# Index scores of a sparse-attention layer: three passes over padded keys become two stacked passes, woven with the strip products

## The chip, the cores and the metric

One core of a Trainium2 chip runs the whole kernel. The metric is the device time of one execution in microseconds (us), from the median of several runs. The tensor engine is TensorE (PE in the profile, its weight loads PEld), the vector engine VectorE (DVE), the scalar engine ScalarE (ACT), the general engine GpSimd (POOL), and SyncE (SP) only issues transfers. SBUF is the on-chip memory, PSUM the accumulators: 8 banks of 512 float32 columns by 128 partitions.

## The reference, cut to what matters

The kernel computes two layers of an encoder for 1024 tokens with a model width of 1024. Layer 1 has sparse attention. An indexer gives each query a score for each key, and the 256 best keys are attended. This document is about the indexer:

```python
q_idx = partial_rope(q_idx.reshape(b, s, IDX_HEADS, IDX_DIM), positions)   # 16 heads x 64
k_idx = partial_rope(k_idx, positions)                                     # one key of 64
idx_logits = relu(einsum('bqhd,bsd->bqhs', q_idx, k_idx))
score = einsum('bqh,bqhs->bqs', w_idx, idx_logits) * IDX_SCALE
score = where(visible, score, -inf)
top_val, top_idx = lax.top_k(score, topk)                                  # topk = 256
```

Each head's 1024 x 1024 logits pass a ReLU, are weighted by a number per query and head, and are summed over 16 heads. The projections ahead of it multiply x (1024 x 1024) with weight strips of 128 columns: 8 strips for `q_idx` (two heads each), one for the key, two for the latent key and value, a narrow one for the weights. After top-k come 32 strips of the attention's own queries ("q strips"), a value projection, and the attention.

## The kernel before, in words

All products are bf16 with float32 accumulation. For accuracy each float32 operand is split into a high bf16 part and a low bf16 rest, and a product is made of three passes: high x high, low x high, high x low. A strip product (`products`, L302) is 8 contraction tiles x 3 passes x 2 halves of 512 columns = 48 matmuls and fills two PSUM banks. Weights come in pieces of 512 KB through four slots: SyncE loads `w_stage`, GpSimd splits it into `w_hi` and `w_lo` (L272, L275), TensorE uses it. The order on each engine is written out by hand, one program per engine and phase, tied by counting semaphores.

Layer 0 is one block of phases. Its last phase ("dn0", down projection and second norm) also computes the small strips of layer 1 (key, two latent strips, weights) while it waits for the norm. Then the semaphores are cleared behind a barrier of all engines (`clear_sems`, L176), and layer 1 is a second block: index, top-k, attention, output projection and norm, feed-forward. In the index phase:

- SyncE loads the rotary tables (L1467) and then the weight pieces of the eight index strips and of the first four q strips.
- ScalarE takes each strip out of PSUM: four copies of 32 rows, exchanged in pairs, into `strip_w` (L1456) and one of 128 rows into `strip_f` (L1457). VectorE multiplies both by the tables and adds them (L1561, L1562, L1565). ScalarE writes the high part (L1533), VectorE the low part (L1584). There is one `strip_f` and one `strip_w`, so the copy of a strip waits for the low part of the strip before.
- The key's high and low parts are held twice, once per head of a strip, each with zeros in the 64 rows of the other head.
- Only when all strips are rotated does TensorE begin the scores. There are 96 steps: 8 strips x 2 heads x 6 query blocks of 128 (blocks 2 to 7; the first two see no more than 256 keys). Block i has (i + 1) x 128 key columns, so 384 to 1024. A step has three passes (L1501) into one of four pairs of banks, a ReLU on ScalarE (L1541) from PSUM into `strip_f` or `strip_w`, and on VectorE one instruction that multiplies by the weight and adds into `score` (L1595). TensorE waits for the ReLU of four steps before, ScalarE for the add of two steps before.
- Strips 1 to 7 of the score steps run in a hardware loop.

In the top-k phase VectorE finds 8 maxima per row and step and replaces them, 32 times (L1786, L1790), and writes the masks `hide`. Beside it TensorE computes the 32 q strips and then 16 value chunks of 6 matmuls (L1688), whose high parts ScalarE and whose low parts VectorE takes out of PSUM (L1739, L1807). A value chunk from the ninth on waits for a low part of an earlier chunk. The first latent scores of the attention (L1872) follow.

## Time and profile before

| | us |
|---|---|
| median of 3 timed runs | 3090.5 |
| lowest and highest | 3088.91 and 3095.48 |
| profiled execution, its time | 3094.27 |
| profiled execution, its span | 3092.5 |
| TensorE busy in the span | 2916.7 (94%) |
| VectorE busy | 1828.5 (59%) |
| ScalarE busy | 1030.8 (33%) |
| GpSimd busy | 1452.6 (47%) |
| mean granted TensorE clock | 0.984 |

The span runs from the first to the last instruction; the execution's time is a little longer. "Busy" is the time with at least one instruction in work. Matmuls are pipelined, so a matmul is shown longer than the distance to the next. The granted clock is a share of full speed: 1.0 is 2.4 GHz and 0.5 is 1.2 GHz, and a mean between them is a mixture. The index phase lies at about 1381 to 1622 us of the span.

### The profile page before, as it was taken

The page shows a single profiled execution, that of the slowest core. Times are in us where ns is not written, and L with a number is a line of the kernel's source. Part 1 is how long each engine was busy: PE and PEld are TensorE (multiplying, and loading weights), DVE is VectorE, ACT ScalarE, POOL GpSimd, SP SyncE. Part 2 cuts the span into 40 slices and gives each one's busy share as a digit, 9 for nine tenths or more (in the row PEclk, how much of TensorE's full clock was granted, in tenths as well). Part 3 has the DMA queues.
Part 4 walks back from the last instruction along what each step waited for, and adds up shares of the span by engine and source line. Part 5 has one row for each costly group of instructions (what it writes and reads, how often), then busy time and mean ns, then how long its engine had stood idle before and what let it go on. Part 6 is the DMA issues. An engine that isn't in the chain of part 4 may idle for free.

```text
span 3092.5 us, 45889 instructions
## 1 busy us (share of the span) xinstructions
PE 2916.7 (94%) x17190; PEld 1514.4 (49%) x17472; DVE 1828.5 (59%) x2540; ACT 1030.8 (33%) x1671; POOL 1452.6 (47%) x721
## 2 busy tenths in 40 slices
PE   7999997999999999977789999999999999999998
PEld 4566655444444444443344444577764444444443
DVE  5877556574444473155589999777757644444042
ACT  3655667022222210014563343566640222221000
POOL 4677211654343378825106777500017534343885
PEclk9999999999999999998899999999999999999999
DMA  4222221411111133311002222111112111111322
GB/s 137 56 65 67 58 59 28 178 55 48 54 47 54 48 109 123 102 36 68 27 0 96 109 102 88 69 55 54 54 68 77 60 54 47 54 47 61 110 96 101
DMA packets 96516, 218.24 MB, mean 71 GB/s; under 512 B 41328, under 2 KB 41456, under 8 KB 96416
## 3 DMA queue, kind: packets, MB, share of 16 engines
q1 hardware_dynamic: 54048, 195.74, 17.9%
q10 hardware_dynamic: 42368, 21.11, 2.9%
q8 instruction: 70, 1.15, 0.1%
q14 instruction: 30, 0.25, 0.0%
HBM read 176.92 MB, written 23.12 MB: 65 GB/s over the span
## 4 chain that ended last, share of the span: by engine, by line
PE 44%; DVE 5%; ACT 4%; issue 1%; POOL 1%; DMA 0%; DVEq 0%; POOLq 0%; ACTq 0%; SPq 0%
PE ps L302 24%; PE ps L313 8%; PE ps L1872 5%; PE ps L1908 2%; DVE score L1595 1%; PE ps L1887 1%; ACT strip_w L1541 1%; PE ps L337 1%; ACT strip_w L1456 1%; PE ps L1688 1%; POOL w_hi L272 0%; DVE strip_f L1565 0%; DVE strip_w L1562 0%; DVE x_res L1224 0%; POOL w_lo L275 0%
## 5 line engine op out<-in xcount | busy, mean ns | idle before, releaser
L272 POOL TENSOR_TENSOR w_hi<-w_stage,ones 128x1024 bf16<-128x1024 f32 x227 | 460.6, 2029 | 908.7 <-PE ps L302 539.9
L302 PE MATMUL ps<-xt_hi,w_hi 128*128 128x512 bf16 x1888 | 566.0, 380 | 33.8 <-ACT strip_f L1457 29.6
L302 PE MATMUL ps<-xt_lo,w_hi 128*128 128x512 bf16 x1889 | 565.7, 380 | 1.6
L302 PE MATMUL ps<-xt_hi,w_lo 128*128 128x512 bf16 x1880 | 563.8, 380 | 2.1
L275 POOL TENSOR_TENSOR w_lo<-w_stage,w_hi 128x1024 bf16<-128x1024 f32 x227 | 525.3, 2314 | 17.8
L302 PEld LDWEIGHTS ps<-xt_hi,w_hi 128*128 128x128 bf16 x1920 | 187.6, 98 | 259.5 <-issue 29.3
L302 PEld LDWEIGHTS ps<-xt_lo,w_hi 128*128 128x128 bf16 x1920 | 187.9, 98 | 227.8 <-issue 1.9
L302 PEld LDWEIGHTS ps<-xt_hi,w_lo 128*128 128x128 bf16 x1920 | 187.8, 98 | 227.4 <-issue 1.1
L1224 DVE SCALAR_TENSOR_TENSOR x_res<-x_res,ps 128x1024 f32<-128x1024 f32 x32 | 38.9, 1216 | 359.5 <-PE ps L313 359.5
L1354 DVE TENSOR_SCALAR conv_up<-gate_up,conv_w_up 128x1024 f32<-128x1024 f32 x44 | 78.4, 1782 | 280.0 <-ACT gate_up L1335 279.4
L313 PE MATMUL ps<-w_hi,hid_hi 128*128 128x512 bf16 x689 | 206.4, 379 | 5.6 <-DVE x_res L1224 4.0
L313 PE MATMUL ps<-w_lo,hid_hi 128*128 128x512 bf16 x690 | 206.6, 379 | 0.7
L313 PE MATMUL ps<-w_hi,hid_lo 128*128 128x512 bf16 x690 | 206.4, 379 | 0.7
L1872 PE MATMUL ps<-lat_hi,q_now 128*128 128x512 bf16 (+3 forms) x729 | 185.6, 323 | 1.2
L1192 ACT ACTIVATE ln_rstd<-ln_rstd 128x1 f32<-128x1 f32 x32 | 6.5, 203 | 524.0 <-DVE ln_rstd L1233 524.0
L1790 DVE MATCH_REPLACE8 score<-best,score 128x384 f32<-128x384 f32 (+2 forms) x192 | 165.7, 876 | 0.0
L1786 DVE MAX8 best<-score 128x8 f32<-128x384 f32 (+2 forms) x192 | 155.5, 879 | 3.3
L1366 DVE TENSOR_TENSOR hid_lo<-conv_up,hid_hi 128x1024 f32 x44 | 115.8, 2633 | 59.5 <-ACT hid_hi L1339 59.5
L898 POOL TENSOR_TENSOR prob<-take,prob 128x1024 f32<-128x1024 f32 (+3 forms) x64 | 107.0, 1677 | 87.5 <-DVE prob L877 71.1
L1996 POOL COPY v_now_hi<-val_hi 128x512 bf16 (+1 forms) x16 | 9.8, 613 | 270.6 <-PE ps L1887 253.3
L694 DVE TENSOR_TENSOR pt_lo<-ps,pt_hi 128x512 bf16<-128x512 f32 x192 | 100.1, 548 | 55.9 <-ACT pt_hi L688 55.7
L673 PE MATMUL ps<-ident,prob 128*128 128x128 f32 x576 | 89.8, 281 | 43.8 <-DVE pt_lo L694 40.5
(230 smaller groups left out, 5757.4 us busy)
## 6 DMA issues: line engine op xcount, KB each, us to landing
w_stage<-in_l_up SPq DMA_DIRECT2D x88, 512.0 KB, 3.2
w_stage<-in_l_down SPq DMA_DIRECT2D x88, 512.0 KB, 3.2
w_stage<-in_l_o SPq DMA_DIRECT2D x32, 512.0 KB, 3.9
w_stage<-in_l_q SPq DMA_DIRECT2D x32, 512.0 KB, 4.6
q_split<-q_out SPq DMA_DIRECT2D x32, 512.0 KB, 2.6
q_now<-q_split SPq DMA_DIRECT2D x16, 1024.0 KB, 4.8
w_stage<-in_l_qkv SPq DMA_DIRECT2D x24, 512.0 KB, 3.3
k_twice<-nk_hi ACTq DMA_DIRECT2D x32, 128.0 KB, 2.9
```

What stands on the lines that cost most here:

```text
L272: pool.tensor_tensor(w_hi[slot][:, 0:cols], w_stage[slot][:, 0:cols], ones[:, 0:1].to_broadcast([P, cols]), ALU.mult).then_inc(w_cast[slot ...
L275: pool.tensor_tensor(w_lo[slot][:, 0:cols], w_stage[slot][:, 0:cols], w_hi[slot][:, 0:cols], ALU.subtract).then_inc(w_split[slot], 1)
L302: mm = pe.matmul(ps[:, bank + h, :], w, a[:, k, h * HALF:(h + 1) * HALF], start=(first and k == k0 and m == 0), stop=(last and k == k1 - 1 ...
L313: mm = pe.matmul(ps[:, bank + h, :], a[:, k, rows], w[slot][:, h * HALF:(h + 1) * HALF], start=(k == 0 and m == 0), stop=(k == tiles - 1 a ...
L673: mm = pe.transpose(dst, self.prob[t % 4][:, cols], ident[:, :])
L694: dve.tensor_tensor(lo, src, hi, ALU.subtract).then_inc(self.lo, 1)
L898: pool.tensor_tensor(prob[t % 4][:, 0:n], take[t % 4][:, 0:n], prob[t % 4][:, 0:n], ALU.mult).then_inc(s_wsb, 1)
L1354: dve.tensor_scalar(conv[a][:, :], gate[a][:, 0:SEQ], tap(0), tap(3), ALU.mult, ALU.add).then_inc(s_cv, 1)
L1366: dve.tensor_tensor(hid_lo[:, m, :], conv[a][:, :], hid_hi[:, m, :], ALU.subtract).then_inc(s_hl, 1)
L1786: dve.max(best[:, c, :], score[:, sc_at[i]:sc_at[i] + span[i]]).then_inc(s_top, 1)
L1790: dve.match_replace(cell, best[:, c, :], cell, TAKEN_SCORE).then_inc(s_rep, 1)
L1872: mm = pe.matmul(ps[:, 2 * (t % 2) + c // 512, 0:w], a, b, start=(kt == 0 and m == 0), stop=(kt == 1 and m == 2))
```

## The change

- The barrier and the clearing of semaphores between the layers go, and both layers are one block. The norms' semaphores are made once and shared, and each norm phase waits for values with its own offset (`at`, `phases_done`). SyncE waits for the sixteenth residual add (`s_acc`) before it loads the tables.
- The exchange of 32-row parts is no longer done by four copies out of PSUM. ScalarE copies the strip once into one of two `strip_f` and then issues four SBUF-to-SBUF transfers from its own queue into one of two `strip_w` (two for the latent strip). The product with the sine table moves to GpSimd. The cosine product and the sum are done by VectorE in the PSUM banks of the strip.
- The key is held once, high and low, with its 64 rows in both halves of the partitions. A query strip is held per head as one tile of 128 rows: the head's 64 high rows in their place and its 64 low rows in the other half. One pass with the key's high part gives high x high + low x high, and a second with the key's low part the rest. Two buffers of query strips stay instead of eight.
- Strips and scores are woven: product s, then the twelve steps of strip s - 2, and so on. The last two groups have q strip 0 between them and q strip 1 behind them. Copy, rotate, highs and lows of a strip stand at set places among the ReLUs and adds of the strip before.
- The strips use banks 4 to 7, the steps banks 0 to 3 in two pairs. ReLU is done in PSUM, the add reads PSUM, and a step's matmuls wait for the add of two steps before. The first six adds write `score` instead of adding to it. Loops are unrolled. `strip_unit` is one of the eight contraction tiles of a strip product, six matmuls as in `products`; `strip_bank(s)` is 4 or 6, and `strip_lows` counts two low parts per strip.
- In the top-k phase the q strips use the banks in the order 4, 6, 0, 2, only strips 2 and 3 are left of the first four, the value chunks' banks are shifted by four for the first eight, and chunk 8 waits for five low parts, chunk 9 for six, and so on.

```diff
+        s_gb, s_blk, s_acc = sem("gb_loaded"), sem("block_done"), sem("accumulated")
-                    pe.wait_ge(s_b, i + 1)
+                    pe.wait_ge(s_b, TB * at + i + 1)
...
-        clear_sems()
...
+        qi = [[room(f"qi{b}{hh}", [P, SEQ], BF16) for hh in range(2)] for b in range(2)]
+        ki_hi, ki_lo = [room(n, [P, SEQ], BF16) for n in ("ki_hi", "ki_lo")]
+        strip_f = [room(f"strip_f{b}", [P, SEQ], F32) for b in range(2)]
+        strip_w = [room(f"strip_w{b}", [P, SEQ], F32) for b in range(2)]
+        IDX_STEPS = 2 * len(picky)
+        Q_BANK = (4, 6, 0, 2)
+        SMALL_LOWS = 3
+        def idx_step(g):
+            s, t = g // IDX_STEPS, g % IDX_STEPS
+            return s, t // len(picky), picky[t % len(picky)], 2 * (g % 2)
...
         def index_sync(sp):
+            sp.wait_ge(s_acc, TB * 2)
         def index_gpsimd(pool):
+            def sine(w, tab, b, swapped):
+                pool.wait_ge(s_sw5[b], swapped)
+                pool.tensor_tensor(w, w, tab, ALU.mult).then_inc(s_s5, 1)
+            split_piece(pool, feed_qidx, 0, 0)
+            pool.wait_ge(s_tl5, 64)
+            sine(strip_w[0][:, :], rope_i[1][:, :], 0, 64)
+            split_piece(pool, feed_qidx, 1, 0)
...
+            for s in range(KT):
+                sine(strip_w[s % 2][:, :], rope_i[1][:, :], s % 2, swaps_through(s))
+                if s < 4:
+                    split_piece(pool, feed_qidx, s, 1)
+                else:
+                    split_piece(pool, feed_q, s - 4, 0)
         def index_tensor(pe):
-                    products(pe, feed_qidx, r, i, 2 * ((r + 1) % 4), xt_hi, xt_lo, 0, KT, True, True)
-                        pe.wait_ge(s_ir, idx_steps * p + t - 3)
-                        for m, (a, b) in enumerate(((qi_hi, ki_hi), (qi_lo, ki_hi), (qi_hi, ki_lo))):
-                                           b[hh][:, c:c + w], start=(m == 0), stop=(m == 2))
+            def scores(g):
+                s, hh, i, bank = idx_step(g)
+                if g % IDX_STEPS == 0:
+                    pe.wait_ge(s_l5, strip_lows(s))
+                if g >= 2:
+                    pe.wait_ge(s_ia, g - 1)
+                for c in range(0, span[i], 512):
+                    w = min(512, span[i] - c)
+                    for m, keys in enumerate((ki_hi, ki_lo)):
+                        mm = pe.matmul(ps[:, bank + c // 512, 0:w], qi[s % 2][hh][:, i * P:(i + 1) * P],
+                                       keys[:, c:c + w], start=(m == 0), stop=(m == 1))
+                mm.then_inc(s_iq, 1)
+            for s in range(KT):
+                if s == 0:
+                    pe.wait_ge(s_l5, 1)
+                elif s == 1:
+                    pe.wait_ge(s_w5, 2)
+                else:
+                    pe.wait_ge(s_l5, strip_lows(s - 2))
+                for k in range(KT):
+                    strip_unit(pe, feed_qidx, s % 4, s // 4, strip_bank(s), k)
+                if s >= 2:
+                    for t in range(IDX_STEPS):
+                        scores(IDX_STEPS * (s - 2) + t)
+            for r in range(2):
+                pe.wait_ge(s_l5, strip_lows(KT - 2 + r))
+                for t in range(IDX_STEPS):
+                    scores(IDX_STEPS * (KT - 2 + r) + t)
+                for k in range(KT):
+                    strip_unit(pe, feed_q, r, 0, Q_BANK[r], k)
         def index_scalar(act):
+            def copy_strip(m, bank, b, heads, used, swapped, rotated):
+                act.wait_ge(*used)
+                wait_if(act, s_sw5[b], swapped)
+                act.activation(strip_f[b][:, :], banks(bank), ACT.Copy).then_inc(s_f5, 1)
+                act.wait_ge(s_f5, m + 1)
+                wait_if(act, s_a5, rotated)
+                for a in range(0, 64 * heads, 32):
+                    to = a + 32 if a % 64 == 0 else a - 32
+                    act.dma_start(strip_w[b][to:to + 32, :], strip_f[b][a:a + 32, :]).then_inc(s_sw5[b], 16)
...
+            def relu(g):
+                s, hh, i, bank = idx_step(g)
+                act.wait_ge(s_iq, g + 1)
+                act.activation(banks(bank)[:, 0:span[i]], banks(bank)[:, 0:span[i]], ACT.Relu).then_inc(s_ir, 1)
+            def highs(s):
+                act.wait_ge(s_a5, 2 + s + 1)
+                if s >= 2:
+                    act.wait_ge(s_iq, IDX_STEPS * (s - 1))
+                for hh in range(2):
+                    rows = slice(hh * IDX_DIM, (hh + 1) * IDX_DIM)
+                    act.activation(qi[s % 2][hh][rows, :], banks(strip_bank(s))[rows, :], ACT.Copy).then_inc(s_h5, 1)
+            for s in range(KT):
+                copy_strip(2 + s, strip_bank(s), s % 2, 2,
+                           (w_used[feed_qidx.slot(s % 4)], feed_qidx.used(s % 4, s // 4) + 1),
+                           swaps_through(s) - 64, s + 1)
+                for t in range(IDX_STEPS):
+                    if s >= 1 and t < 5:
+                        relu(IDX_STEPS * (s - 1) + t)
+                    if t == 4:
+                        highs(s)
+                    if s >= 1 and t >= 5:
+                        relu(IDX_STEPS * (s - 1) + t)
+            for t in range(IDX_STEPS):
+                relu(IDX_STEPS * (KT - 1) + t)
         def index_vector(dve):
+            def cosine(m, bank, rows, tab):
+                src = banks(bank)[0:rows, :]
+                dve.wait_ge(s_f5, m + 1)
+                dve.tensor_tensor(src, src, tab[0:rows, :], ALU.mult).then_inc(s_c5, 1)
+            def rotate(m, bank, rows, b):
+                src = banks(bank)[0:rows, :]
+                dve.wait_ge(s_c5, m + 1)
+                dve.wait_ge(s_s5, m + 1)
+                dve.tensor_tensor(src, src, strip_w[b][0:rows, :], ALU.add).then_inc(s_a5, 1)
...
+            def add(g):
+                s, hh, i, bank = idx_step(g)
+                cell, src = score[:, sc_at[i]:sc_at[i] + span[i]], banks(bank)[:, 0:span[i]]
+                w = w_idx[:, i, 2 * s + hh:2 * s + hh + 1]
+                dve.wait_ge(s_ir, g + 1)
+                if g < len(picky):
+                    dve.tensor_scalar(cell, src, w, None, ALU.mult).then_inc(s_ia, 1)
+                else:
+                    dve.wait_ge(s_ia, g - len(picky) + 1)
+                    dve.scalar_tensor_tensor(cell, src, w, cell, ALU.mult, ALU.add).then_inc(s_ia, 1)
+            def lows(s):
+                for hh in range(2):
+                    rows = slice(hh * IDX_DIM, (hh + 1) * IDX_DIM)
+                    other = slice((1 - hh) * IDX_DIM, (2 - hh) * IDX_DIM)
+                    dve.wait_ge(s_h5, SMALL_LOWS + 2 * s + hh + 1)
+                    dve.tensor_tensor(qi[s % 2][hh][other, :], banks(strip_bank(s))[rows, :],
+                                      qi[s % 2][hh][rows, :], ALU.subtract).then_inc(s_l5, 1)
+            for s in range(KT):
+                cosine(2 + s, strip_bank(s), P, rope_i[0])
+                for t in range(IDX_STEPS):
+                    if t == 3:
+                        rotate(2 + s, strip_bank(s), P, s % 2)
+                    if t == 7:
+                        lows(s)
+                    if s >= 1:
+                        add(IDX_STEPS * (s - 1) + t)
+            for t in range(IDX_STEPS):
+                add(IDX_STEPS * (KT - 1) + t)
...
+        def chunk_bank(c):
+            return (c + Q_BANK[0]) % 8 if c < 8 else c % 8
...
-            pe.wait_ge(s_ir, idx_steps * KT)
-                products(pe, feed_q, r, 0, 2 * r, xt_hi, xt_lo, 0, KT, True, True)
+            pe.wait_ge(s_ia, IDX_STEPS * KT)
+            for r in range(2, 4):
+                products(pe, feed_q, r, 0, Q_BANK[r], xt_hi, xt_lo, 0, KT, True, True)
+                    products(pe, feed_q, r, i, Q_BANK[r], xt_hi, xt_lo, 0, KT, True, True)
-                    pe.wait_ge(s_vl, c - 7)
+                    pe.wait_ge(s_vl, (c + Q_BANK[0]) % 8 + 1)
...
```

## Rows read from the trace of the kernel before

**Rows 1.** Busy time of each engine, granted clock and transfers in five stretches.

```profile
core 0: us, PE busy (x) PEld busy (x) DVE busy (x) ACT busy (x) POOL busy (x), PEclk, DMA share, GB/s
1381.20:1409.60 28.40, 0.00 (x1) 0.14 (x3) 18.82 (x11) 10.24 (x10) 17.49 (x7) 0.50 0.52 176
1409.60:1496.60 87.00, 85.05 (x382) 38.17 (x388) 42.74 (x30) 40.68 (x42) 36.13 (x16) 0.99 0.15 52
1496.60:1519.60 23.00, 3.70 (x12) 1.47 (x14) 9.62 (x8) 12.35 (x14) 3.33 (x2) 0.59 0.07 23
1519.60:1621.80 102.20, 91.60 (x458) 43.15 (x467) 87.15 (x96) 70.48 (x95) 0.00 (x0) 0.97 0.00 0
1621.80:1974.30 352.50, 351.08 (x1603) 159.35 (x1629) 340.66 (x607) 134.23 (x141) 243.21 (x110) 1.00 0.26 98
```

**Rows 2.** Chain of waits, 1370 to 1660 us: start, duration, work on it.

```profile
1383.77 6.92 DMA rope_q_sin<-rope_tables
...
1402.89 2.82 DVE ki_lo L1571
...
1409.60 11.61 PE ps L302 x47
...
1606.66 1.03 ACT strip_w L1541
1607.83 1.30 DVE score L1595
...
1619.33 1.03 ACT strip_w L1541
1620.41 10.04 PE ps L302 x38
```

**Rows 3.** Timeline of TensorE at the end of the value chunks: start, duration.

```profile
1974.11 0.38 PE L1688 MATMUL ps<-w_lo,lat_hi 128*128 128x512 bf16 x1
1974.33 0.38 PE L1872 MATMUL ps<-lat_hi,q_now 128*128 128x512 bf16 x1
```

**Rows 4.** ReLU (L1541), add (L1595) and residual add (L1224): durations in ns.

```profile
L1541 ACT ACTIVATE strip_f<-ps x48: 485/704/922, 1519.0 to 1618.1; 128x384 f32<-128x384 f32 x16, 128x640 f32<-128x640 f32 x16, 128x896 f32<-128x896 f32 x16
L1541 ACT ACTIVATE strip_w<-ps 128x1024 f32<-128x1024 f32 x16 | 16.4, 1024 | 8.4 <-DVE score L1595 6.8 <-PE ps L1501 1.6
L1595 DVE SCALAR_TENSOR_TENSOR score<-strip_w,w_idx,score x48: 744/1018/1287, 1520.2 to 1620.5; 128x512 f32<-128x512 f32 x16, 128x768 f32<-128x768 f32 x16, 128x1024 f32<-128x1024 f32 x16
L1224 DVE SCALAR_TENSOR_TENSOR x_res<-x_res,ps 128x1024 f32<-128x1024 f32 x32 | 38.9, 1216 | 359.5 <-PE ps L313 359.5
```

**Rows 5.** Transfers inside SBUF from ScalarE's queue: length of the issue, and landing.

```profile
L626 ACTq DMA_DIRECT2D k_twice<-nk_hi x32: 617/620/1867, 50.7 to 493.4; - x32
k_twice<-nk_hi ACTq DMA_DIRECT2D x32, 128.0 KB, 2.9
```

**Rows 6.** GpSimd by line and shape: count, busy us, mean ns.

```profile
L275 POOL TENSOR_TENSOR w_lo<-w_stage,w_hi 128x1024 bf16<-128x1024 f32 x226 | 524.9, 2323 | 17.8
L272 POOL TENSOR_TENSOR w_hi<-w_stage,ones 128x1024 bf16<-128x1024 f32 x226 | 459.2, 2032 | 908.7 <-PE ps L302 539.9 <-PE ps L313 227.7 <-PE ps L569 48.3
L1755 POOL TENSOR_TENSOR qs_w<-qs_w,rope_q_sin 64x1024 f32<-64x1024 f32 x16 | 37.6, 2352 | 193.9 <-ACT qs_w L1718 193.9
```

**Rows 7.** The stretches 502 to 538 us by engine, as rows 1.

```profile
502.00:510.00 8.00, 4.42 (x32) 3.19 (x34) 5.70 (x15) 7.55 (x18) 0.00 (x0) 1.00 0.00 1
510.00:514.00 4.00, 1.22 (x12) 0.84 (x9) 3.48 (x10) 3.75 (x10) 0.00 (x0) 1.00 0.41 66
514.00:518.00 4.00, 3.81 (x12) 1.81 (x14) 2.31 (x6) 1.95 (x5) 0.00 (x0) 0.57 0.00 0
524.00:538.00 14.00, 7.46 (x53) 5.23 (x55) 10.63 (x30) 13.42 (x32) 0.00 (x0) 1.00 0.00 1
```

**Rows 8.** Timeline of VectorE at the end of top-k.

```profile
1959.64 0.19 DVE L1803 MEMSET hide<- 64x64 bf16 x2
1959.75 4.44 DVE L1807 TENSOR_TENSOR val_lo<-ps,val_hi 128x512 bf16<-128x512 f32 x7
```

More of the change, by code:

```diff
@@ L1046, in back_and_norm @@
             b_rows = room(f"b_rows_{tag}", [P, D_MODEL], F32)
[L1047 to L1054 removed]
+            s_x = [sem(f"{tag}_x_loaded{g}") for g in range(2)] if load_x is not None else None
+            at = phases_done(tag)
+            s_out = sem(f"{tag}_stored") if final is not None else None
             tail = tiles - SLOTS
@@ L1449, in copy_strip @@
-        def copy_strip(act, bank, kind, wait_prev):
-            act.wait_ge(s_l5, wait_prev)
-            src = banks(bank)
-            swaps = {"idx": (0, 32, 64, 96), "lat": (0, 32), "plain": ()}[kind]
-            for a in swaps:
-                b = a + 32 if a % 64 == 0 else a - 32
-                act.activation(strip_w[b:b + 32, :], src[a:a + 32, :], ACT.Copy)
-            act.activation(strip_f[:, :], src, ACT.Copy).then_inc(s_f5, 1)
-        def strip_kind(m):
-            return "idx" if m == 0 or m >= 3 else ("lat" if m == 1 else "plain")
+        s_sw5 = [sem(f"strip_swapped{b}") for b in range(2)]
@@ new lines, in strip_unit @@
+        def strip_unit(pe, feed, n, i, bank, k):
+            slot = feed.slot(n)
+            if k == 0:
+                pe.wait_ge(w_split[slot], feed.use(n, i) + 1)
+            wh, wl = w_hi[slot][:, k * P:(k + 1) * P], w_lo[slot][:, k * P:(k + 1) * P]
+            for m, (w, a) in enumerate(((wh, xt_hi), (wh, xt_lo), (wl, xt_hi))):
+                for h in range(2):
+                    mm = pe.matmul(ps[:, bank + h, :], w, a[:, k, h * HALF:(h + 1) * HALF],
+                                   start=(k == 0 and m == 0), stop=(k == KT - 1 and m == 2))
+            if k == KT - 1:
+                mm.then_inc(w_used[slot], 1)
@@ new lines, in index_scalar, with low @@
+            for t in range(IDX_STEPS):
+                relu(IDX_STEPS * (KT - 1) + t)
+        def index_vector(dve):
+            def cosine(m, bank, rows, tab):
[7 more added lines that the diff above has]
+                dve.tensor_tensor(src, src, strip_w[b][0:rows, :], ALU.add).then_inc(s_a5, 1)
+            def low(dst, hi, bank, n):
+                dve.wait_ge(s_h5, n)
+                dve.tensor_tensor(dst, banks(bank), hi, ALU.subtract).then_inc(s_l5, 1)
+            dve.wait_ge(s_tl5, 64)
+            cosine(0, 0, P, rope_i[0])
+            cosine(1, 2, ROPE, rope_q[0])
+            low(lat_lo[:, 1, :], lat_hi[:, 1, :], 4, 1)
+            rotate(0, 0, P, 0)
+            rotate(1, 2, ROPE, 1)
+            low(ki_lo[:, :], ki_hi[:, :], 0, 2)
+            low(lat_lo[:, 0, :], lat_hi[:, 0, :], 2, 3)
+            dve.wait_ge(s_w5, 2)
+            def add(g):
[26 more added lines that the diff above has]
+                add(IDX_STEPS * (KT - 1) + t)
@@ L2022, in program @@
         run_phases(
+            *layer0,
             phase(index_sync, index_gpsimd, index_tensor, index_scalar, index_vector),
```

222 lines of the change are left out of this document (57 added, 165 removed).

## The prediction, made before the changed kernel had run

> **What bounds the kernel now.** I read the stage table of the index part first [rows 1]. TensorE has nothing to multiply from 1381.2 to 1409.6 us, works on the eight index products until 1496.6, stands for most of the next 23 us, and runs the 96 score steps until about 1619. Then come 352.5 us in which TensorE (the q strips) and VectorE (top-k) are both busy throughout. The chain of waits says why [rows 2]: the hole at 1381 is the table loads, issued only after the barrier, then the rotation of the key strip through one pair of SBUF buffers (the last low half is written at 1402.89 to 1405.7), and the first product only starts at 1409.60. The score steps are not limited by TensorE: ReLU and add follow each other, and twelve steps take 1619.33 - 1606.66 = 12.67 us.
>
> **Prices.** A 512-column matmul starts every 0.216 us and is shown 0.38 long [rows 3], so 0.165 is its tail. A product of 48 is 10.36 us. A ReLU is 0.485 us at 384 elements and 1.024 at 1024, linear between; the add is 1.285 at 1024 and 0.744 at 512 [rows 4]. Between engines 0.05 us passes where no register is stepped (1619.33 + 1.03 to 1620.41) and 0.11 to 0.14 where the loop does it [rows 2]. The new code has constants only, so I take 0.2 for the three hand-overs of a step (matmul to ReLU to add to matmul).
>
> **The change, part by part.**
>
> *The start.* No barrier, and the tables are loaded after the last residual add of the stage before, some 40 us earlier, so tables, weight pieces and the small strips' copies lie beside the small products. SyncE's queue holds only these loads and is moved past nothing else. On GpSimd the key strip's sine stands between the first two splits, which take 2.0 + 2.3 us each [rows 6]; with the first slot free from the small product at 1368 both are ready before products 0 and 1 need them at 1381 and 1392. Product 0 starts at 1381.2, where TensorE falls idle now. Gain: 28.4 us.
>
> *The first strip.* Product 2 waits for the low half of strip 0. From the end of product 0: copy 1.02, four DMA issues on ScalarE at 0.62 = 2.5, landing 2.9 [rows 5], sine on GpSimd 2.35 [rows 6], rotate 1.2, two highs 2.0, two lows 2.4, waits 0.4: 14 us. Product 1 covers 10.4 of them, so 3.6 are open. 1381.2 + 20.7 + 3.6 + 10.4 (product 2) = 1416.0, where the first group starts.
>
> *A group of twelve steps.* Passes go from three to two, and the stacked copies make the zero halves unnecessary. For TensorE a group is 2 x 8448 columns / 512 x 0.216 = 7.1 us, against 10.7 now. But banks fall from four to two: a step's matmuls wait for the add of two steps before, since ReLU and add now work in the bank itself. Behind that wait stand the rest of the group and the next product, and for these wait the copy of the next strip and everything after it. So one bank is a closed ring of matmul, ReLU and add. The odd bank has the larger sizes (512, 768, 1024, twice): matmuls 1.94 + 3 x 0.165 = 2.44, ReLUs 2.43, adds 3.05, waits 0.6, together 8.5, twice 17.0; the last ReLU and add (2.4) run beside the next product, which leaves 14.8. Inside the group lie a rotate on VectorE, two highs on ScalarE and two lows on VectorE of the following strip. Walked step by step, the rotate holds the add of step 3 back by 1.0 us, the highs hold the ReLU of step 5 by 0.6, the lows, which wait for the highs, the add of step 7 by 1.3. A group is 14.8 + 2.9 = 17.7 us, in which TensorE works 7.1. The four DMA issues, copy, cosine, sine and split fall into the product that follows and are hidden by its 10.4 us. GpSimd's splits don't slow the adds: the residual add, one input in PSUM, has 1216 ns on average over 32 with GpSimd busy beside many of them [rows 4].
>
> *The sum to the last add.* 1416.0; five times group and product, 5 x 28.05 = 140.3, 1556.3; group 5, 17.7; group 6 follows without a product, so the copy with its four DMA issues and the late sine of strip 7 are open: 17.7 + 5.1 = 22.8; q strip 0, 10.4; group 7 without insertions 14.8, 1622.0; last ReLU and add 2.4: 1624.4. Now it is 1620.5 + 1.29 = 1621.8 [rows 4]. So the hole at the start is given back inside the groups: a strip costs 28 us where product and steps cost 10.9 + 12.7 now.
>
> The norms' semaphores, now shared by both layers, change constants only and cost nothing.
>
> *Bounds of what rows 4 don't show.* An add that reads PSUM with a weight per partition: 1285 (SBUF, same form) or 1216 (PSUM, constant factor) at 1024. The lower one would give 4.4 us over all groups; I take the middle, 1622.2. A ReLU that writes PSUM is shown nowhere: the nearest is the same one into SBUF (1.024); lower bound is its column part alone, 0.86, upper bound the SBUF figure plus as much. I take 1.024.
>
> The Trainium skill, "VectorE: DVE Perf Modes", section on the TRN2 errata, gives VectorE a larger fixed cost for a PSUM source than for SBUF (120 against 58 cycles). That would be an estimated 65 ns per add and put the last add 2 us later. The trace does not bear it out: 1216 ns from PSUM against 1285 from SBUF.
>
> *The clock.* Over a whole group TensorE is shown busy 7.1 + 12 x 0.165 = 9.1 of 17.7 us. At such a share (7.46 of 14 us, 4.42 of 8) the granted clock stayed 1.00 [rows 7]. But around the lows (steps 6 to 8) it is 1.8 of 6 us, and after 1.22 of 4 us the clock was 0.57 [rows 7], so at 1.2 instead of 2.4 GHz for most of the stretch. I expect one fall per group. One fall costs what it costs at 1409.60: 11.61 us for a product of 10.36 [rows 2], 1.25 us. Eight are 10 us: last add at 1632.2.
>
> The Trainium skill, "TensorE: Matmul & The Clock Gate", section "HAM oscillation", says that dependence gaps in a loop return the clock to half each time round. That speaks against this change; the trace agrees with it in the fall after 1.22 of 4 us.
>
> *Top-k and values.* VectorE needs 1959.8 - 1621.8 = 338.0 us from the last add to the end of the hide masks [rows 8]. Before, TensorE ended last here (32 strips, 16 value chunks) and VectorE had some slack. Now two q strips are done early (one before and one behind the last group), so TensorE reaches value chunk 8 at 1629.7 + 31 x 10.36 + 8 x 1.295 = 1961. It waits there, as chunk 8 now takes the bank of chunk 4 and needs five lows of VectorE: 1632.2 + 338.0 + 5 x 0.634 [rows 8] = 1973.4. Eight chunks are 10.4, plus 1.5 for the clock after 12 us without work: the first latent score starts at 1985.3, where it is 1974.33 [rows 3]. Its order behind that point is the same. Difference: +11 us. The profiled execution has 3094.3 us (span 3092.5 and 1.8 around it), so 3105; it lay 3.8 above the median of the three timed runs, 3090.5. On their scale I forecast 3101.
>
> **The rivals.** 0.2% (6 us) is about what a measurement of this kernel can tell from no change.
> - *The clock holds* (chance 0.20): for it, 524 to 538 [rows 7]; against it, the 30% around the lows. Last add 1622.2, first latent score 1975.3, +1: 3091.5.
> - *Faster: the ring is shorter than SBUF rows say* (0.16). Place: ReLU and add of every step, both in PSUM. If the ReLU were at its lower bound and the add at 1216, and the clock held because the ring is shorter, the last add would be at 1613.7, first latent score at 1966.8, -7.5: 3083. It decides from a last add before about 1615. Against it: nothing in the rows is that short. The Trainium skill, "ScalarE: Activation LUTs", section "Step-by-step: what each stage is for", says that ScalarE writes PSUM faster than SBUF. It gives no figure, and no row here shows such a write; this rival is what it would bring at most.
> - *The clock stays at half through the groups* (0.12): all step matmuls at double length put the last add at 1648.7, and the sum at +28: 3118. Against it: busy shares of half held 1.00.
>
> **Numbers.** The forecast has 0.52 (own range 3096 to 3110). Slower by over 0.2%: forecast and third rival, less the lower edge, 0.60; within: 0.23; faster: 0.17. The range 3086 to 3114 leaves out part of the faster case and of the slowest.
>
> **What would show it.** Right: product 0 within 2 us of 1381; a repeat of about 28 to 29.5 us per strip; a score step's matmul released by VectorE's add; granted clock at half inside groups (mean under 0.9 over the stage); last add at 1628 to 1636; TensorE idle some 10 us in the value chunks. Wrong: a repeat under 27 us (ring too dear), clock at 1.00 throughout, a hole left at 1381, or a ReLU in PSUM well under 1.0 us.

## The result, and the profile after

The changed kernel takes 3107.61 us (median of 6 runs, 3103.43 to 3110.55) against 3094.88 us (6 runs, 3088.91 to 3095.85, the three of the table above among them) for the kernel before: a ratio of 1.0043, 95% interval 1.0030 to 1.0056. The ratio is an estimate over all runs; the two medians alone give 1.0041. The kernel is slower, by less than half a percent but clear of noise. The forecast was 3101.0, in a range of 3086 to 3114.

The profiled execution took 3108.03 us (span 3106.2, mean granted clock 0.977).

In what follows "product s" is the 48 matmuls of strip s, and a "group" is the twelve score steps of one strip; groups count from 0.

**One offset first.** The first normalization of layer 0, long before any changed work of the index stage, starts 3.3 us later in the profiled execution after than in that before. In the fourteen executions of this study (before, after, twelve experiments) this row starts between 577.2 and 586.0. With one profiled execution of the kernel before, nothing shows whether part of the 3.3 us belongs to the change. So I take 3.3 us off each time of the changed kernel ("aligned") and give the last add of each experiment as a distance from this row. Timeline of VectorE, first the kernel before, then the changed one; the row holds min, median and max in ns, then first and last start:

```profile
L1228 DVE BATCH_NORM_STATS2 ln_stats_o<-x_res x8: 676/685/695, 581.6 to 590.9; 128x6 f32<-128x512 f32 x8
```

```profile
L1222 DVE BATCH_NORM_STATS2 ln_stats_o<-x_res x8: 676/685/695, 584.9 to 594.2; 128x6 f32<-128x512 f32 x8
```

**By stretches** of the changed kernel, columns as in [rows 1]: small products' end; products 0 to 2; groups 0 to 4 with products 3 to 7; groups 5 to 7 with q strip 0; then q strips and top-k up to the first latent score.

```profile
1381.20:1384.70 3.50, 3.30 (x101) 2.87 (x100) 1.51 (x2) 1.19 (x3) 3.42 (x3) 1.00 0.00 0
1384.70:1419.67 34.97, 32.62 (x141) 14.32 (x143) 10.54 (x9) 6.30 (x8) 21.94 (x11) 0.95 0.30 91
1419.67:1566.17 146.50, 108.24 (x432) 43.41 (x440) 78.34 (x80) 58.63 (x75) 29.14 (x14) 0.83 0.13 36
1566.17:1637.40 71.23, 48.26 (x177) 17.58 (x180) 41.60 (x43) 32.51 (x43) 8.80 (x5) 0.76 0.08 22
1637.40:1987.05 349.65, 339.89 (x1542) 154.22 (x1572) 336.69 (x608) 133.13 (x140) 242.68 (x110) 0.99 0.26 99
```

The hole of [rows 1], 1381 to 1409, is gone: TensorE is busy 3.30 of the first 3.50 us and goes straight on. In its place the two stretches with the groups stand at a mean clock of 0.83 and 0.76, and a strip costs (1566.17 - 1419.67) / 5 = 29.3 us. A group, a product and a group in full, and the last group, which has nothing inserted:

```profile
1419.67:1439.26 19.59, 12.64 (x41) 4.42 (x41) 13.24 (x14) 9.69 (x13) 0.00 (x0) 0.66 0.08 27
1439.26:1449.64 10.38, 10.33 (x48) 4.59 (x47) 2.42 (x2) 2.03 (x2) 4.04 (x2) 0.99 0.22 51
1449.64:1468.26 18.62, 10.58 (x41) 3.88 (x41) 12.61 (x14) 9.70 (x13) 2.29 (x2) 0.82 0.08 28
1620.58:1635.04 14.46, 8.92 (x42) 3.19 (x41) 9.81 (x11) 7.85 (x11) 0.00 (x0) 1.00 0.00 1
```

Group 6, which follows group 5 with no product between them, ran at half clock for nearly its whole length:

```profile
1589.70:1610.20 20.50, 13.01 (x35) 4.36 (x37) 13.38 (x14) 9.64 (x13) 6.32 (x3) 0.50 0.15 43
```

What TensorE waited for between 1384.7 and 1640 (us in total, times, longest):

```profile
PE ps L1502 <- DVE score L1615: 55.6, 45, 3.0
PE ps L1502 <- DVE score L1612: 4.6, 4, 1.8
PE ps L1458 <- DVE qi L1622: 2.2, 1, 2.2
```

In a group, the score matmuls (L1502) are released by VectorE's add (L1615), not by the product or by ScalarE. The longest of these waits, 3.0 us, lies across the two lows (L1622, the subtractions that write the low parts of the next strip). There the clock falls. In TensorE's timeline of group 1 a 512-column matmul is 0.38 long before the wait (2.4 GHz) and 0.63 after it (1.2 GHz):

```profile
1456.48 0.38 PE L1502 MATMUL ps<-ki_lo,qi 128*128 128x512 bf16 x1
1457.06 0.33 PE L1502 MATMUL ps<-ki_lo,qi 128*128 128x384 bf16 x1
1460.41 0.63 PE L1502 MATMUL ps<-ki_lo,qi 128*128 128x512 bf16 x1 [3.02 <-DVE score L1615]
1460.83 0.63 PE L1502 MATMUL ps<-ki_hi,qi 128*128 128x512 bf16 x1
```

The durations that answer [rows 4] (ReLU now inside PSUM, add now from PSUM) and [rows 5] (the swap DMAs: issue, then landing):

```profile
L1556 ACT ACTIVATE ps<-ps x96: 471/742/1008, 1420.2 to 1635.1; 128x384 f32<-128x384 f32 x16, 128x512 f32<-128x512 f32 x16, 128x640 f32<-128x640 f32 x16, 128x768 f32<-128x768 f32 x16
...
L1556 ACT ACTIVATE ps<-ps 128x1024 f32<-128x1024 f32 x16 | 16.1, 1008 | 9.5 <-PE ps L1502 9.2
...
L1615 DVE SCALAR_TENSOR_TENSOR score<-ps,w_idx,score x90: 606/945/1285, 1430.0 to 1636.1; 128x384 f32<-128x384 f32 x15, 128x512 f32<-128x512 f32 x15, 128x640 f32<-128x640 f32 x15, 128x768 f32<-128x768 f32 x15
...
L1535 ACTq DMA_DIRECT2D strip_w<-strip_f x32: 514/612/620, 1396.1 to 1589.6; - x32
...
strip_w<-strip_f ACTq DMA_DIRECT2D x32, 128.0 KB, 2.3
```

The end of top-k, answering [rows 8] and [rows 3]. VectorE:

```profile
1968.80 2.70 DVE L1834 TENSOR_SCALAR hide<-score 128x384 bf16<-128x384 f32 x6
1971.46 0.18 DVE L1842 MEMSET hide<- 64x64 bf16 x2
1971.57 4.80 DVE L1846 TENSOR_TENSOR val_lo<-ps,val_hi 128x512 bf16<-128x512 f32 x8
```

TensorE, from value chunk 8 to the first latent score:

```profile
1974.63 0.61 PE L1728 MATMUL ps<-w_hi,lat_hi 128*128 128x512 bf16 x1 [8.08 <-DVE val_lo L1846]
1975.04 0.63 PE L1728 MATMUL ps<-w_hi,lat_lo 128*128 128x512 bf16 x1
...
1987.05 0.38 PE L1911 MATMUL ps<-lat_hi,q_now 128*128 128x512 bf16 x1
```

### The profile page after: what moved, and what is told of

Read it like the earlier page. It is cut to its first block, busy times and chain, and to the rows that moved or that the text cites. A ratio compares the mean times of both kernels' runs of the same rounds, so it can differ in the third digit from the quotient of the medians.

```text
span 3106.2 us, 44954 instructions
## 1 busy us (share of the span) xinstructions
PE 2917.3 (94%) x17027; PEld 1503.7 (48%) x17312; DVE 1798.8 (58%) x2531; ACT 996.9 (32%) x1639; POOL 1467.1 (47%) x731
## 3 DMA queue, kind: packets, MB, share of 16 engines
q1 hardware_dynamic: 54048, 195.74, 17.7%
## 4 chain that ended last, share of the span: by engine, by line
PE 71%; DVE 17%; issue 4%; ACT 3%; POOL 3%; ACTq 2%; DMA 1%; DVEq 0%; POOLq 0%
PE ps L292 27%; PE ps L303 17%; PE ps L1911 5%; DVE best L1825 5%; DVE score L1829 5%; PE ps L553 5%; PE ps L327 3%; PE ps L1458 2%; PE ps L1947 2%; PE ps L663 2%; PE ps L559 1%; PE ps L1502 1%; PE ps L748 1%; PE ps L1926 1%; POOL w_hi L262 1%
## 5 line engine op out<-in xcount | busy, mean ns | idle before, releaser
L265 POOL TENSOR_TENSOR w_lo<-w_stage,w_hi 128x1024 bf16<-128x1024 f32 x227 | 520.1, 2291 | 17.8
L292 PE MATMUL ps<-xt_hi,w_hi 128*128 128x512 bf16 x1732 | 517.4, 379 | 1.5
L292 PE MATMUL ps<-xt_lo,w_hi 128*128 128x512 bf16 x1726 | 516.1, 379 | 1.8
L292 PE MATMUL ps<-xt_hi,w_lo 128*128 128x512 bf16 x1722 | 515.2, 379 | 2.0
L292 PEld LDWEIGHTS ps<-xt_hi,w_hi 128*128 128x128 bf16 x1760 | 172.2, 98 | 207.7
L292 PEld LDWEIGHTS ps<-xt_lo,w_hi 128*128 128x128 bf16 x1760 | 172.2, 98 | 207.6
L292 PEld LDWEIGHTS ps<-xt_hi,w_lo 128*128 128x128 bf16 x1760 | 172.2, 98 | 207.6
L1615 DVE SCALAR_TENSOR_TENSOR score<-ps,w_idx,score 128x384 f32<-128x384 f32 (+2 forms) x90 | 83.1, 947 | 93.3 <-ACT ps L1556 93.0
```

The source lines that it names most:

```text
L265: pool.tensor_tensor(w_lo[slot][:, 0:cols], w_stage[slot][:, 0:cols], w_hi[slot][:, 0:cols], ALU.subtract).then_inc(w_split[slot], 1)
L292: mm = pe.matmul(ps[:, bank + h, :], w, a[:, k, h * HALF:(h + 1) * HALF], start=(first and k == k0 and m == 0), stop=(last and k == k1 - 1 ...
```

## The experiments

"Last add" is its start less the start of the layer 0 row above; it is 1038.9 before and 1051.2 after. "Strip" is the distance of one strip's work from the next one's, as a mean over five: from the first score matmul of group 0 to that of group 5. Where the product lies inside the groups (e1, e5, e6, e7, e10, e12) it goes by the first ReLU, from group 1 to group 6. Each ratio is to the kernel before, run on the same chip; times "by the ratios" are their differences times 3095 us. The intervals are 3 to 6 us wide to either side, so a difference of a few us between two rows isn't clear of noise.

| run | ratio (95% interval) | strip, us | last add |
|---|---|---|---|
| changed kernel | 1.0043 (1.0030 to 1.0056) | 29.3 | 1051.2 |
| e1_fill | 0.9894 (0.9875 to 0.9912) | 23.5 | 1007.3 |
| e2_relu_sbuf | 0.9946 (0.9929 to 0.9962) | 26.4 | 1026.4 |
| e3_third_pass | 1.0055 (1.0036 to 1.0074) | 30.3 | 1060.6 |
| e4_keep_busy | 1.0013 (1.0004 to 1.0023) | 28.2 | 1043.2 |
| e5_fill_sync | 0.9896 (0.9878 to 0.9914) | 23.5 | 1007.6 |
| e6_fill_relu_sbuf | 0.9843 (0.9826 to 0.9861) | 21.8 | 991.9 |
| e7_fill_both | 0.9837 (0.9818 to 0.9857) | 21.4 | 990.5 |
| e8_late_tables | 1.0112 (1.0093 to 1.0132) | | 1066.8 |
| e9_early_insert | 1.0059 (1.0043 to 1.0075) | 29.7 | 1059.2 |
| e10_both_later | 0.9892 (0.9871 to 0.9912) | 23.7 | 1005.6 |
| e11_tables_behind | 1.0090 (1.0073 to 1.0108) | | 1066.8 |
| e12_both_apart | 0.9871 (0.9850 to 0.9892) | 22.7 | 999.6 |

**The clock and the ring (e4, e3).** e4 fills TensorE's waits inside groups 0 to 5 with extra matmuls. They add into the bank of the strip's product, whose last unit moves behind the group, so its scores aren't the reference's:

```diff
+        EXTRA = (0, 3, 0, 4, 4, 0, 12, 0, 7, 0, 2, 0)
...
-                for k in range(KT):
+                for k in range(KT - (s >= 2)):
                     strip_unit(pe, feed_qidx, s % 4, s // 4, strip_bank(s), k)
                 if s >= 2:
                     for t in range(IDX_STEPS):
                         scores(IDX_STEPS * (s - 2) + t)
+                        for h in range(EXTRA[t]):
+                            pe.matmul(ps[:, strip_bank(s) + h % 2, :], ident_b[:, :], xt_hi[:, 0, 0:HALF],
+                                      start=False, stop=False)
+                    strip_unit(pe, feed_qidx, s % 4, s // 4, strip_bank(s), KT - 1)
```

> In six of the eight groups extra matmuls of 512 columns fill TensorE's waits (32 in a group, 6.9 us; they accumulate into the strip's own bank, whose last k-unit follows the group, so the strips' values differ from the reference's). Theory A (the clock's falls cost 1.25 to 1.5 us per group): granted clock near 1.00 from 1420 to 1570, groups 17.4 to 18 us, the kernel 6 to 9 us faster than the changed one: about 3100. Rival B (the falls lie in the waits and cost nothing; groups are long for other reasons): clock up, groups still 18.6 to 19.6, 3106 to 3109. Rival C (the extra matmuls themselves delay steps): groups longer, 3112 or more.

Theory A. Two of its groups, 1414 to 1432 and 1443 to 1460 us, and one group with its product:

```profile
1414.44:1432.25 17.81, 15.37 (x71) 6.14 (x72) 13.03 (x14) 9.69 (x13) 1.35 (x1) 1.00 0.10 30
1442.61:1460.40 17.79, 15.55 (x72) 6.14 (x72) 13.01 (x14) 9.69 (x13) 2.73 (x2) 1.00 0.09 30
...
1414.44:1442.61 28.17, 25.68 (x118) 10.84 (x120) 15.76 (x16) 11.73 (x15) 4.95 (x3) 1.00 0.15 38
```

At full clock a group is 17.8 us and a strip 28.17, where the forecast's walk gave 17.7 and 28.05. The groups of the changed kernel are 18.6 to 19.6. The last add comes 8.0 us earlier, and the time falls from 1.0043 to 1.0013 of the kernel before, 9 us; the two intervals don't meet. So the falls of the clock cost what the forecast says, and they are most of the 13 us by which the changed kernel is slower: without those that e4 removes it is 4 us behind the kernel before.

e3 adds a third pass to each score step, the low keys a second time, so its scores aren't the reference's either:

```diff
-                    for m, keys in enumerate((ki_hi, ki_lo)):
+                    for m, keys in enumerate((ki_hi, ki_lo, ki_lo)):
```

> Adds a third pass to every score step (the low keys are added a second time, so the scores differ from the reference's). Theory A (TensorE's matmuls lie inside the ring, so passes cost although TensorE is idle most of a group): the larger steps 512, 768 and 1024 of each half add 0.97 us, 1.9 per group at full clock, up to 3.9 where the clock is at half; eight groups 15 to 30 us, 3123 to 3137. Rival B (TensorE has 9 us of idle time in a group, the pass goes into it): 3106 to 3110.

Neither. A strip grew by 1.0 us, not 1.9 to 3.9. The last add is 9.4 us later, in an execution that was the slowest of four (3118.1 against a median of 3113.7); by the ratios e3 is 3.7 us slower, which isn't clear of noise. The groups take 19.5 to 20.5 us, the walk plus 1.9 at full clock would be 19.6. So the extra pass pays for about half of what it puts into the ring. The likely reason is the clock, 0.93 over groups 0 to 4 where the changed kernel has 0.83; no run separates it.

```profile
1419.75:1571.32 151.57, 118.70 (x531) 51.47 (x541) 79.22 (x80) 58.84 (x75) 29.13 (x14) 0.93 0.13 35
```

**The block of the product (e1), and what comes late next (e5).**

```diff
+            def filled(s, unit):
+                k = 0
+                for t in range(IDX_STEPS):
+                    scores(IDX_STEPS * s + t)
+                    for _ in range((1, 1, 0, 1, 1, 0, 1, 1, 0, 1, 1, 0)[t]):
+                        unit(k)
+                        k += 1
...
-                for k in range(KT):
-                    strip_unit(pe, feed_qidx, s % 4, s // 4, strip_bank(s), k)
-                if s >= 2:
-                    for t in range(IDX_STEPS):
-                        scores(IDX_STEPS * (s - 2) + t)
+                if s < 2:
+                    for k in range(KT):
+                        strip_unit(pe, feed_qidx, s % 4, s // 4, strip_bank(s), k)
+                else:
+                    filled(s - 2, lambda k: strip_unit(pe, feed_qidx, s % 4, s // 4, strip_bank(s), k))
...
```

> The eight k-units of a strip's product (and of the two early q strips) no longer stand as a block ahead of a group of twelve score steps; one unit of six matmuls (1.3 us) follows each of the steps 0, 1, 3, 4, 6, 7, 9 and 10. Theory A (a group is a ring of matmul, ReLU and add that leaves TensorE without work for more than half its time, and nothing needs the product earlier): the units go into the waits. A strip then costs the ring, 17.7 to 19 us, plus what ScalarE does between two groups (strip copy 1.0, four DMA issues 2.4), 20 to 22.5 us where it is 29.3 now; the granted clock stays near 1.00; last add 55 to 65 us earlier than 1637.4, and as TensorE's q strips follow it, the whole kernel 50 to 60 us faster: about 3053. Rival B (the units stand ahead of score matmuls in TensorE's order, so each delays the ring by its 1.3 us and nothing is won but the clock): repeat 27 to 29 us, 3095 to 3108.

Theory A's mechanism, but short of its size: 23.5 us a strip instead of 20 to 22.5, the last add 43.9 us earlier instead of 55 to 65, and by the ratios 46 us faster than the changed kernel. The clock is 1.00 through the stage:

```profile
1420.00:1560.00 140.00, 111.10 (x515) 47.34 (x524) 93.62 (x96) 69.86 (x90) 37.97 (x18) 1.00 0.17 45
```

In e5 SyncE issues the swap DMAs (the four `dma_start` calls move from `copy_strip` to `index_sync`, where they stand between the weight loads).

> e1 (product units between the steps) with the four swap DMAs of each strip issued by SyncE instead of ScalarE. e1 repeats every 23 us per strip, and ScalarE's copy and its four issues (4 x 0.61) stand between the last ReLU of a group and the first of the next. Theory A (these issues lie in the ring between groups): repeat 20.5 to 21.3, last add 14 to 18 us earlier than in e1, 3044 to 3049. Rival B (in e1 the issues are hidden, because the scores of the next group are ready and a unit follows): repeat 22.5 to 23, 3058 to 3062. Rival C (SyncE stands at a weight load when a swap is due, the rotation comes late): slower than e1, over 3064.

The time is rival B's, its reason is not, and rival C is out: the issues begin 0.03 us after the copy's end, as on ScalarE. In e1 the four issues did stand in the ring: ScalarE's ReLUs waited 15.1 us for "issue", six times 2.5. In e5 that is gone, and VectorE waits 13.6 us at the rotate for GpSimd's sine (e1: 3.9). The chain from the copy's end to the sine's end takes 6.6 us in both runs, so the likely reading is that without the issues VectorE only comes to the rotate earlier: one wait took the place of the other. Waits of 1420 to 1560 us, first e1, then e5:

```profile
ACT ps L1561 <- issue: 15.1, 6, 2.5
...
DVE ps L1595 <- POOL strip_w L1476: 3.9, 6, 0.7
```

```profile
DVE ps L1604 <- POOL strip_w L1490: 13.6, 6, 2.3
```

**ReLU in SBUF (e2, e6, e7).** e2 undoes the "ReLU in PSUM" part alone:

```diff
-                    pe.wait_ge(s_ia, g - 1)
+                    pe.wait_ge(s_ir, g - 1)
...
-                act.activation(banks(bank)[:, 0:span[i]], banks(bank)[:, 0:span[i]], ACT.Relu).then_inc(s_ir, 1)
+                if g >= 2:
+                    act.wait_ge(s_ia, g - 1)
+                act.activation(relu_f[g % 2][:, 0:span[i]], banks(bank)[:, 0:span[i]], ACT.Relu).then_inc(s_ir, 1)
...
```

> Undoes one part: ReLU writes one of two SBUF tiles again and a bank pair is free for the matmuls once its ReLU is done; the two bank pairs, the two passes and the order stay. Theory A (the ring through the add is what makes a group 18.6 to 19.6 us): now VectorE sets the group: adds 10.4, rotate 1.2, two lows 2.4 and hand-overs, 15 to 16 us; repeat 25.5 to 26.5 us, last add about 25 us earlier, 3082. Rival B (the rotate, highs and lows of the next strip and the ring of two buffers between ReLU and add set it as much): repeat 28.5 to 29.3, 3102 to 3108.

Theory A: groups of 15 to 17 us, a strip of 26.4, the last add 24.8 us earlier. By the ratios the kernel is 30 us faster than the changed one and 17 us faster than before. So the ReLU in PSUM alone cost more than the whole loss: with two bank pairs, a bank that is held until the add closes the ring. The other parts together are a gain. Whether one of them costs too wasn't separated; a ReLU in PSUM with the four bank pairs of the kernel before, which would say how much of the ring is the small number of banks, wasn't run.

> e1 with e2: units between the steps, ReLU into SBUF, bank free after the ReLU. Theory A (both act on different waits: e2 took 2.9 us off a strip's 29.3, e1 took the product off it): repeat 20 to 21 us, 3038 to 3046. Rival B (once the units lie between the steps they set the distance of steps, and the release of the bank is no longer the last wait): repeat 22.5 to 23, 3056 to 3062.

> e1, e2 and e5 together. Theory A: TensorE's own work, 7.1 + 10.4 = 17.5 us per strip, or VectorE's 15.2 and hand-overs, is what is left: repeat 17.6 to 19 us; last add 30 to 40 us earlier than in e1, 3020 to 3032. Rival B (rotation of the next strip, 14 us from copy to lows, comes late once a strip takes under 20 us): repeat 20 to 21, 3038 to 3046.

e6 (e1 and e2) is 16 us faster than e1. It lies just outside theory A (3047.6 us and a strip of 21.8, against 3038 to 3046 and 20 to 21). e7 (with e5 too) has the lowest time, 1.63% under the kernel before, but it can't be told from e6. Its time is rival B's, a strip (21.4) is a little over rival B's 20 to 21, and VectorE's wait at the rotate is up to 2.8 us a strip (16.7 us, six times).

**Where the next strip's steps stand (e9, e10, e12).** e9 takes the changed kernel and moves rotate, highs and lows from steps 3, 5 and 7 to 0, 0 and 2:

```diff
-                    if t == 3:
+                    if t == 0:
                         rotate(2 + s, strip_bank(s), P, s % 2)
-                    if t == 7:
+                    if t == 2:
                         lows(s)
...
```

> The changed kernel with the next strip's rotate, highs and lows moved: rotate and highs ahead of step 0 of a group, lows ahead of add 2 (now: step 3, 5 and 7). Theory A (my 2.9 us per group for these insertions, as they hold ReLUs and adds back): at the head of a group they lie mostly beside the product (sine done 7.6 us after the product's start, rotate 1.2, highs 2.0: 10.8 of 10.5), only the lows' 2.4 delay an add, part of it in VectorE's own waits; group 16 to 17 us, and fewer falls of the clock; repeat 27 to 28 where it is 29.3, 3092 to 3102. Rival B (the group is ring-bound everywhere, an insertion costs the same wherever it stands): 3105 to 3109. Rival C (the rotation comes too late for step 0 and its wait opens a hole in the head of each group): slower, over 3112.

Rival C by the time (3115.4 us) and by the wait, though the difference from the changed kernel, 5 us by the ratios, isn't clear of noise. ScalarE stood 8.0 us at the highs with the group's first ReLU behind them, because the sine ends only at 1447.1, 8.8 us after the product's start at 1438.3 (I had put 7.6), and rotate and highs follow one another. Yet a strip grew by only 0.4 us, as nothing was inserted further inside the group any more. Of the 8.1 us by which the last add is late, some 6 arise behind the start of group 5, where groups 5 and 6 follow each other and no product covers the rotation. ScalarE's timeline at the head of group 1:

```profile
1448.52 2.06 ACT L1564 ACTIVATE qi<-ps 64x1024 bf16<-64x1024 f32 x2 [7.96 <-DVE ps L1588]
1450.60 0.97 ACT L1556 ACTIVATE ps<-ps 128x384 f32<-128x384 f32 x2
```

> e7 with rotate ahead of add 6 instead of 3, highs ahead of ReLU 7 instead of 5, lows ahead of add 9 instead of 7. In e7 VectorE stands 2.8 us at the rotate, because copy, swap and sine of the strip are not through by step 3, and every strip takes about 21 us. Theory A (that wait is the last one above TensorE's 17.5 us): repeat 18 to 19.5, last add 10 to 20 us earlier, 3024 to 3034. Rival B (the later lows hold back the next group's first scores): repeat 20.5 to 21.5, 3040 to 3047.

> e7 with rotate ahead of add 5 (there 3), highs ahead of ReLU 8 (5), lows ahead of add 10 (7). In e7 VectorE stands 2.8 us at each rotate for the sine and a strip takes 21.15 us. e10 moved the rotate to 6 but the highs to 7, one step behind it, and then ScalarE stood 3.4 us at the highs with ReLU 7 behind them. Theory A (what costs is the distance in steps between a rotate and the highs behind which ReLUs stand, since ScalarE runs one or two steps ahead of VectorE; with three steps between nothing stands): the wait at the rotate falls from 2.8 to about 1, repeat 18.5 to 20 us, 3025 to 3037. Rival B (the order copy, swap, sine, rotate, highs, lows is too long for a group, whatever the places): repeat 21 to 23.5, 3043 to 3062.

e10 is slower than either theory had it (3061.3 us; rival B said 3040 to 3047), and slower than e7 by 17 us. VectorE's wait at the rotate is gone in it, but ScalarE's at the highs is 18.7 us, six times up to 3.4. In e12 both are gone, and it is still 10 us slower than e7 by the ratios (the intervals just overlap), with its last add 9.1 us later. That is rival B's range (3056.7 us, a strip of 22.7): e12's theory A had it that nothing else would cost. Two things differ from e7: TensorE waits 7.0 us for the later lows, and 90 adds take 115.5 us where e7 has 98.8. e6 has 110.2 for them and yet a strip of 21.8, so the adds alone don't explain it; how the two shares divide stays open. That the adds are stretched is plain. The 640-column adds of the changed kernel, from PSUM (count, busy us, mean ns):

```profile
L1615 DVE SCALAR_TENSOR_TENSOR score<-ps,w_idx,score 128x640 f32<-128x640 f32 x15 | 13.2, 879 | 6.6 <-ACT ps L1556 6.6
```

And of e12, from SBUF, first all 90 (min, median and max in ns):

```profile
L1630 DVE SCALAR_TENSOR_TENSOR score<-relu_f,w_idx,score x90: 605/1012/3110, 1421.8 to 1585.6; 128x384 f32<-128x384 f32 x15, 128x512 f32<-128x512 f32 x15, 128x640 f32<-128x640 f32 x15, 128x768 f32<-128x768 f32 x15
...
L1630 DVE SCALAR_TENSOR_TENSOR score<-relu_f,w_idx,score 128x640 f32<-128x640 f32 x15 | 21.8, 1456 | 14.8 <-ACT relu_f L1573 14.8
```

In e12 the stretched adds stand beside GpSimd's sine and splits. Of its 90 adds, the 70 with no GpSimd instruction beside them take at most 1.02 times what the same size takes in the kernel before, and the other 20 take 2.5 times it on average. In e2, e6, e7 and e10, where the add reads SBUF too, the adds alone are never stretched either (at most 1.02). In the changed kernel 13 adds out of PSUM have GpSimd beside them and keep their time (at most 1.02). In one place three adds (640, 768, 896) take 6.61 us, where the same sizes take 3.04 from PSUM (0.88 + 1.01 + 1.15), and GpSimd is busy beside them. VectorE, then GpSimd:

```profile
1458.18 6.61 DVE L1630 SCALAR_TENSOR_TENSOR score<-relu_f,w_idx,score 128x640 f32<-128x640 f32 x3 [0.17 <-ACT relu_f L1573]
```

```profile
1458.56 2.72 POOL L1491 TENSOR_TENSOR strip_w<-strip_w,rope_i_sin 128x1024 f32<-128x1024 f32 x1 [16.37 <-DMA strip_w<-strip_f]
1461.23 2.61 POOL L262 TENSOR_TENSOR w_hi<-w_stage,ones 128x1024 bf16<-128x1024 f32 x1
```

**The start (e8, e11).** Both load the rotary tables only when the small products are done (`sp.wait_ge(w_used[3], ...)` ahead of the loads). In e8 the weight loads stand behind that wait too; e11 issues the first four of them ahead of it.

> The changed kernel, but the rotation tables are loaded only when the last small product is done (as the barrier made it before); double buffers, DMA swaps and order stay. Theory A (the early loads are what brings product 0 forward): tables land 3 to 5 us after the small products, two cosines and a low follow: product 0 starts 7 to 9 us late and the whole kernel is 7 to 10 us slower, 3115 to 3118; the other 20 us of the gain of 28.4 at the start come from the rest (weights, no barrier, two buffers). Rival B (nearly all 28 us hang on the tables): 3130 or more. Rival C (the group ring hides a late start): 3106 to 3109.

> As e8, but the first four weight loads are issued ahead of the late tables, so that only the tables are late. In e8 the weights stood behind the tables on SyncE and the second product waited 13.5 us for its split weights. Theory A (e8's 20 us were mostly this): tables land 4 to 6 us after the small products; product 0 starts 7 to 9 us late and the first strip's chain a few more: 3115 to 3121. Rival B (GpSimd's queue, where the key strip's sine stands ahead of the second split, passes the tables' lateness on in full): 3124 to 3129, as e8.

The last add is 15.6 us late in both (times: 21 and 15 us by the ratios, a difference within the noise). So the order of the loads hardly matters, and the lateness of the tables does. e8 lies between its two theories, with theory A too small; e11 lies between its theory A and its rival B. The 13.5 us that e8's TensorE waited for split weights came ahead of its first index product and not, as the text recorded for e11 says, its second. In e11 the last table is there 7.9 us after the small products, not 4 to 6; two cosines and a low follow, so the first product waits 11.8 us. Then GpSimd, whose queue holds the key's sine ahead of the second split, passes some more on: TensorE's wait ahead of product 2 is 4.7 us where it was 2.2.

```profile
PE ps L1458 <- DVE lat_lo L1595: 11.8, 1, 11.8
PE ps L1458 <- DVE qi L1623: 4.7, 1, 4.7
PE ps L1458 <- issue: 0.2, 1, 0.2
```

About half of the 28 us of the start are thus the early tables (15.6 us when they alone are late); the rest (two buffers, DMA swaps, no barrier) wasn't separated.

## Why the prediction was right

- *Start.* Product 0 at 1384.70, aligned 1381.4 (forecast 1381.2).
- *First strip.* The hole ahead of product 2 is 2.2 us, not 3.6. The terms listed for this chain add up to 14.8 us, not 14, which would have left 4.4 open; but issues and landings overlap, so that the last swap has landed 4.2 us after the copy's end, where the forecast had 2.5 + 2.9. The clock fell there too, and product 2 took 12.05 (1407.62 to 1419.67) instead of 10.4. The first group starts at 1416.4 aligned (1416.0). That this is so near is luck: errors of either sign cancel.
- *Group.* 17.7 us without the clock's falls: e4 shows 17.8. The inserted steps cost 3.3 instead of 2.9, as a group without them took 14.46 (14.8; the terms listed, 17.0 less 2.4, give 14.6).
- *Clock.* Forecast: one fall in each of eight groups, 1.25 us. Groups 0 to 4 were 18.6 to 19.6, and e4, which fills six groups, prices their falls at 8 to 9 us; so some 1.4 each. Group 7 had none (clock 1.00), and in group 6 the fall lasted 20.5 us: groups 5 and 6 together took 44.1 us, where the forecast with two falls is 43.0. The strip, 29.3, is what the forecast gives with the clock in it (28.05 + 1.25). The Trainium skill's rule ("TensorE: Matmul & The Clock Gate", section "HAM oscillation"), weighed before, is borne out by the clock's return to half in each of groups 0 to 6.
- *PSUM prices.* The ReLU is 1008 ns at 1024 columns against 1024 in SBUF: 16 ns. The add is 1285, as from SBUF; my middle value of 1250 was wrong by 2 us over the stage. The Trainium skill's remark that ScalarE writes PSUM faster holds in sign, and by 16 ns it gives the rival built on it nothing to stand on.
- *Last add.* Ends at 1637.4, aligned 1634.1 (1632.2).
- *Top-k.* From the last add to the masks' end 334.2 us, not 338.0: the six hide masks took 2.70 us, where the kernel before has 6.57 for them. There GpSimd's low halves of the q strip (1953.90 to 1958.60) ran beside them; in the changed kernel these were over at 1960.55, eight us before the masks. This is the term that I carried over unexamined, and it gave back 3.8 us.
- *Values.* Chunk 8 waited 8.1 us, not 12, and the clock was at half for its first 4 us. First latent score at 1987.05, aligned 1983.8 (1985.3): +9.4 us against before where I had +11.
- *Sum.* The span grew by 13.7: 3.3 of offset, 9.4 from there to the first latent score, 1.0 behind it. The medians differ by 12.7 (forecast 10.5); of the 6.6 us between 3101.0 and 3107.6, 4.4 are that the kernel before has a median of 3094.9 over six runs and not 3090.5. How near the sum is owes something to cancelling: last add 1.9 us later than forecast, top-k 3.8 shorter.

One sentence of the working holds only for an add that reads PSUM: "GpSimd's splits don't slow the adds". It doesn't hold for one that reads SBUF (e12).

## What to carry to other kernels

Freeing a buffer only after the last of three engines makes a closed ring; count what stands in it, and count the buffers, before counting the passes that are saved. If an engine waits inside such a ring, put its other work between the steps rather than ahead of them: that alone turned +0.4% into -1.1%, and the clock stayed at 1.00 as well. When a wait is removed and the time stays, look at once for the next one in the same chain, as e5, e10 and e12 show.

## What the runs showed of the hardware

- A VectorE add with both large inputs in SBUF is stretched beside GpSimd's tensor operations, up to 3.1 us where 0.6 to 1.3 is usual; with one input in PSUM the longest of 90 is 1285 ns. The Trainium skill, "SBUF — State Buffer", section "Who interferes with whom", says that a VectorE instruction with two SBUF inputs contends with a GpSimd instruction that reads SBUF, and that the port pair they share is an exclusive lock. The trace agrees that they contend (1456 ns mean against 879 for 640 columns); whether a lock is behind it no run here shows.
- More work for TensorE can cost less than its own length: in e3 a pass of 3.6 us a strip cost 1.0. Part of it went into waits, and the granted clock was 0.93 instead of 0.83.
- A 128 KB transfer inside SBUF from ScalarE's queue costs ScalarE 0.61 us per issue, 2.5 us per strip, and lands 2.3 us after its issue.
